# Two softmax attentions: attention values for two heads at once with V stationary, the result laid out by feature, and the divisors widened by GpSimd and turned by TensorE

## What is computed

```python
def _dsa_attention(...):            # layer 0, 8 heads; k_sel and v_sel are the 128 keys chosen for a query
    logits = jnp.einsum('bqhd,bqkhd->bhqk', qb, k_sel).astype(jnp.float32) * (dh ** -0.5)
    logits = jnp.where(valid[:, None], logits, -jnp.inf)
    p = jax.nn.softmax(logits, axis=-1).astype(v.dtype)
    return jnp.einsum('bhqk,bqkhd->bqhd', p, v_sel).reshape(bsz, Q_BLOCK, h * dh)
```

## Time and profile before

| | |
|---|---|
| three runs | 1926.04, 1927.58, 1929.67 us, median 1927.58 |
| profiled execution: own time | 1927.2 us |
| profiled execution: span | 1925.5 us |
| PE, PEld busy | 1843.1 and 1490.8 us |
| DVE, ACT, POOL busy | 892.6, 744.9 and 618.5 us |
| first attention | 839.8 to 887.6 us of the span |
| second attention | 1391.5 to 1510.2 us of the span, its eight turned tiles included |

### The profile page before, as it was taken

How to read it: one execution, slowest core, us unless ns; L and a number is a source line. 1 busy time by engine, 2 the same in 40 slices (tenths; PEclk the granted TensorE clock), 3 DMA queues, 4 the chain that set the end, 5 groups by cost and what they waited for, 6 DMA issues and landing times.

```text
span 1925.5 us, 22691 instructions
## 1 busy us (share of the span) xinstructions
PE 1843.1 (96%) x9025; PEld 1490.8 (77%) x9025; DVE 892.6 (46%) x1341; ACT 744.9 (39%) x1236; POOL 618.5 (32%) x203
## 2 busy tenths in 40 slices
PE   7999999998989999999999999998999999999998
PEld 4887777676777767878878888877778887888886
DVE  6411466555947258953442223345266253223334
ACT  3324655444334243344432222236544343232232
POOL 1433222222114323411434434334300243344332
PEclk8999999998999999999999999999999999999999
DMA  7533231211131312311222232322300122222321
GB/s 281 202 109 99 66 88 35 77 54 56 45 109 51 120 45 85 101 45 55 74 102 87 90 106 87 100 87 75 109 1 1 55 88 88 100 97 87 108 89 77
DMA packets 83379, 165.11 MB, mean 86 GB/s; under 512 B 5977, under 2 KB 8158, under 8 KB 83294
## 3 DMA queue, kind: packets, MB, share of 16 engines
q1 hardware_dynamic: 83294, 163.95, 25.9%
HBM read 157.64 MB, written 2.10 MB: 83 GB/s over the span
## 4 chain that ended last, share of the span: by engine, by line
PE 87%; DVE 7%; ACT 3%; issue 1%; POOL 1%; DMA 0%; SPq 0%; DVEq 0%; ACTq 0%
PE PDT L622 13%; PE PDT L624 12%; PE PDT L623 12%; PE PDT L633 9%; PE PDT L635 9%; PE PDT L634 9%; PE PM L1201 3%; PE PM L975 2%; PE PM L1171 1%; PE PDT L1171 1%; PE PM L942 1%; PE PM L1150 1%; PE PM L990 1%; PE PM L668 1%; PE PDT L760 1%
## 5 line engine op out<-in xcount | busy, mean ns | idle before, releaser
L1787 POOL TENSOR_TENSOR wlo<-wraw,whi 128x2048 fp32r<-128x2048 f32 (+4 forms) x154 | 606.6, 3945 | 1272.7 <-ACT whi L1304 1232.5
L1304 ACT ACTIVATE whi<-wraw 128x2048 fp32r<-128x2048 f32 (+2 forms) x133 | 247.8, 1863 | 554.1 <-PE PDT L624 320.4
L633 PE MATMUL PDT<-hhi,whi 128*128 128x512 f32 x800 | 316.2, 395 | 5.0 <-ACT mh_r L1423 5.0
L635 PE MATMUL PDT<-hhi,wlo 128*128 128x512 f32 x800 | 313.0, 391 | 0.0
L634 PE MATMUL PDT<-hlo,whi 128*128 128x512 f32 x800 | 313.0, 391 | 0.0
L622 PE MATMUL PDT<-whi,hhi 128*128 128x512 f32 (+1 forms) x612 | 242.9, 397 | 7.5 <-DVE hlo L1892 5.3
L623 PE MATMUL PDT<-wlo,hhi 128*128 128x512 f32 (+1 forms) x612 | 236.2, 386 | 0.0
L624 PE MATMUL PDT<-whi,hlo 128*128 128x512 f32 (+1 forms) x612 | 236.1, 386 | 0.0
L622 PE MATMUL PDT<-whi,mh_hi 128*128 128x512 f32 x512 | 202.5, 396 | 0.0
L624 PE MATMUL PDT<-whi,mh_lo 128*128 128x512 f32 x512 | 202.5, 396 | 0.0
L623 PE MATMUL PDT<-wlo,mh_hi 128*128 128x512 f32 x512 | 202.4, 395 | 0.0
(11 more groups left out here) (344 smaller groups left out, 2507.0 us busy)
## 6 DMA issues: line engine op xcount, KB each, us to landing
wraw<-in_mlp_w SPq DMA_DIRECT2D x64, 1024.0 KB, 5.2
wraw<-in_w_in SPq DMA_DIRECT2D x26, 1024.0 KB, 5.2
wraw<-in_even_w_in SPq DMA_DIRECT2D x16, 1024.0 KB, 5.3
w_ada<-in_w_ada SPq DMA_DIRECT2D x12, 1024.0 KB, 14.0
wraw<-in_w_out SPq DMA_DIRECT2D x8, 1024.0 KB, 5.1
swapped<-qk_sb SPq DMA_DIRECT2D x16, 256.0 KB, 6.6
wraw<-in_even_w_out SPq DMA_DIRECT2D x4, 1024.0 KB, 5.1
wraw<-in_odd_w_o SPq DMA_DIRECT2D x4, 1024.0 KB, 5.2
```

The costliest lines, as they stand in the source:

```text
L633: mm(bank, sth, hi[:, k0 + k, :], start=start and k == 0, stop=False)
L635: last = mm(bank, stl, hi[:, k0 + k, :], start=False, stop=stop and k == 3)
L1304: nc.scalar.activation(whi[base % 2][:, 0:n], wraw[base % 2][:, 0:n], ACT.Copy).then_inc(S("w_hi"), 1)
L1787: part = g.tensor_tensor(wlo[base % 2][:, cols], wraw[base % 2][:, cols], fl(whi[base % 2][:, cols]), ALU.subtract)
```

## The change

In both softmax attentions V is now the stationary operand, 64 columns of it, and the turned probabilities move. Two heads of a pair write partitions 0 to 63 and 64 to 127 of `PM` bank 3, so that a pair's result is already a feature tile of 512 tokens. A pair takes eight products: those of key tiles 1, 3 and 2 in an odd iteration h (`pair_values` with keys 1, 3, 2), that of key tile 0 (512 columns) in the next one. `turn_probs` puts the ten blocks in another order, four `prt` buffers take the place of two.

The divisors: DVE inverts `den` (`invert`), GpSimd spreads each over 64 columns (`widen`), four PE transposes turn a pair's (`turn_den`), ACT copies them to SBUF (`turned_den`), and DVE multiplies `PM` bank 3 by them (`over_den`), once a pair. `lat_high` (ACT) and `lat_low` (DVE) make `hhi` and `hlo` of the pair's tile. The turning of the result after each loop (`transposes`, `split_tiles`) goes. On ACT the copy of the turned probabilities comes after the first two of a head's four exponentials, not after all four. The load of `row_b` for layer 1 is moved behind the second attention, where one `prt` buffer now uses its place.

```diff
+    prt3 = [arena(f"prt3{s}", [P, 1280], kb) for s, kb in enumerate((21, 91, 96))]
+    prt3.append(at("prt33", [P, 1280], offset=place["row_a"]))
@@ -1181,29 +1196,39 @@
 
             X = PX[n % 2]
             pe.wait_ge(S("att_exps"), 4 * n + 4)
-            at_block = 0
             for t in (3, 2, 0, 1):
                 for j in range(t + 1):
-                    last = nc.tensor.transpose(X[:, at_block // 4, (at_block % 4) * P:(at_block % 4) * P + P],
-                                               p[n % 2][:, QB_FIRST[t] + j * P:QB_FIRST[t] + j * P + P], ident[:, :])
-                    at_block += 1
+                    at_column = KEY_FIRST[j] + (t - j) * P
+                    b, c0 = at_column // SEQ, at_column % SEQ
+                    a = QB_FIRST[t] + j * P
+                    last = nc.tensor.transpose(X[:, b, c0:c0 + P], p[n % 2][:, a:a + P], ident[:, :])
             last.then_inc(S("att_turned"), 1)
...
-        def values(n, pt, v):
-
-            c0 = 256 * (n % 2)
-            probs_taken(n + 1)
-            if n:
-                pe.wait_ge(S("att_out"), n)
+        def turn_den(pair, wide):
+
+            pe.wait_ge(S("den_wide"), 2 * pair + 2)
+            pe.wait_ge(S("tr_read"), den_group(pair))
             for t in range(TT):
-                for j in range(t + 1):
-                    a = QB_FIRST[t] + j * P
-                    last = mm(PM[:, 3, c0 + t * HD:c0 + t * HD + HD], pt[n % 2][:, a:a + P], v(j),
-                              start=j == 0, stop=j == t)
-            last.then_inc(S("att_pv"), 1)
+                last = nc.tensor.transpose(PDT[:, 3, t * P:t * P + P], wide[pair % 2][:, t, :], ident[:, :])
+            last.then_inc(S("tr_done"), 1)
+
+        def pair_values(pair, first, keys, pt, v):
+
+            if keys[0]:
+                probs_taken(2 * pair + 2)
+                if pair:
+                    pe.wait_ge(S("att_out"), pair)
+            for s in keys:
+                a, w = KEY_FIRST[s], SEQ - s * P
+                for half in range(2):
+                    c0 = (2 * (pair - first) + half) * HD
+                    last = mm(PM[HD * half:HD * half + HD, 3, s * P:SEQ], v[:, s, c0:c0 + HD],
+                              pt[(2 * pair + half) % 4][:, a:a + w], start=s == 1, stop=s == 0, skip_group_check=True)
+            if keys[0] == 0:
+                last.then_inc(S("att_pv"), 1)
 
...
+            if h >= 3 and h % 2:
+                pair_values((h - 3) // 2, 0, (1, 3, 2), prt, v2)
+                turn_den((h - 3) // 2, den_wide)
+            elif h >= 4:
+                pair_values((h - 4) // 2, 0, (0,), prt, v2)
...
         pe.wait_ge(S("conv2_done"), 4)
         wo2 = pieces("wo2", 1)
-        piece(*wo2[0])
-        pe.wait_ge(S("att_out"), A_H)
-        for n in range(3):
-            transposes("attn", n + 1 + n // 2, lambda t, k: v2[:, t, k * P:k * P + P], n)
-            piece(*wo2[n + 1])
-        transposed("attn", 4)
+        pe.wait_ge(S("tr_read"), TR["den2"][0] + A_H // 2)
+        for p in wo2[:4]:
+            piece(*p)
+        pe.wait_ge(S("attn_low"), KT + A_H // 2)
         for p in wo2[4:]:
             piece(*p)
...
             if n >= 4:
-                act.wait_ge(S("att_out"), n - 3)
-            for q, t in enumerate((3, 2, 0, 1)):
+                act.wait_ge(S("den_wide"), n - 3)
+            for q, t in order:
@@ -1689,19 +1717,36 @@
 
         def turned(n, pt):
             act.wait_ge(S("att_turned"), n + 1)
-            if n >= 2:
-                act.wait_ge(S("att_pv"), n - 1)
-            nc.scalar.activation(pt[n % 2][:, 0:SEQ], PX[n % 2][:, 0, :], ACT.Copy).then_inc(S("probs_s"), 1)
-
-        for h in range(A_H + 1):
+            if n >= 4:
+                act.wait_ge(S("att_pv"), n // 2 - 1)
+            nc.scalar.activation(pt[n % 4][:, 0:SEQ], PX[n % 2][:, 0, :], ACT.Copy).then_inc(S("probs_s"), 1)
+
+        def turned_den(pair):
+
+            act.wait_ge(S("tr_done"), den_group(pair) + 1)
+            if pair >= 2:
+                act.wait_ge(S("attn_low"), KT + pair - 1)
+            nc.scalar.activation(lat[pair % 2][:, :], PDT[:, 3, :], ACT.Copy).then_inc(S("tr_read"), 1)
+
+        def lat_high(pair, k):
+
+            act.wait_ge(S("att_out"), pair + 1)
+            nc.scalar.activation(hhi[:, k, :], lat[pair % 2][:, :], ACT.Copy).then_inc(S("attn_high"), 1)
...
-        for h in range(C_H + 1):
...
             if h < C_H:
-                exps(A_H + h, pr3, mx3, den3)
-            if h:
-                turned(A_H + h - 1, prt3)
+                exps(n, pr3, mx3, den3, ((0, 3), (1, 2)))
+            if 1 <= h <= C_H:
+                turned(n - 1, prt3)
+            if h < C_H:
+                exps(n, pr3, mx3, den3, ((2, 0), (3, 1)))
+            if h >= 5 and h % 2:
+                lat_high((n - 5) // 2, (h - 5) // 2)
+            if h >= 3 and h % 2 and h < C_H + 3:
+                turned_den((n - 3) // 2)
         hi(0, PH["wo3"][0] + 1, 0)
-        split_tiles("lat", 8, lambda k: 1.0, 0, "wo3")
...
+        def widen(n, d, wide):
+
+            pair, c0 = n // 2, HD * (n % 2)
+            pool.wait_ge(S("den_ready"), n + 1)
+            if pair >= 2:
+                pool.wait_ge(S("tr_done"), den_group(pair - 2) + 1)
+            g.tensor_copy(wide[pair % 2][:, :, c0:c0 + HD], d[:, n % 4, :].unsqueeze(2).to_broadcast([P, TT, HD]))\
+                .then_inc(S("den_wide"), 1)
+
+        for n in range(A_H):
+            widen(n, den, den_wide)
...
+        def invert(n, d):
+
             dve.wait_ge(S("att_exps"), 4 * n + 4)
-            link(v.reciprocal(d[:, n % 4, :], d[:, n % 4, :]))
-            dve.wait_ge(S("att_pv"), n + 1)
-            v.tensor_tensor(dst, PM[:, 3, 256 * s:256 * s + 256].rearrange("p (t d) -> p t d", t=TT),
-                            d[:, n % 4, :].unsqueeze(2).to_broadcast([P, TT, HD]), ALU.mult).then_inc(S("att_out"), 1)
-
-        dve.wait_ge(S("causal_made"), 2)
-        for h in range(A_H + 2):
+            v.reciprocal(d[:, n % 4, :], d[:, n % 4, :]).then_inc(S("den_ready"), 1)
+
+        def over_den(pair):
+
+            dve.wait_ge(S("att_pv"), pair + 1)
+            dve.wait_ge(S("tr_read"), den_group(pair) + 1)
+            o = lat[pair % 2][:, :]
+            v.tensor_tensor(o, PM[:, 3, :], o, ALU.mult).then_inc(S("att_out"), 1)
+
+        def lat_low(pair, k):
+
+            dve.wait_ge(S("attn_high"), KT + pair + 1)
+            v.tensor_tensor(hlo[:, k, :], lat[pair % 2][:, :], fl(hhi[:, k, :]), ALU.subtract).then_inc(S("attn_low"), 1)
...
-        for h in range(C_H + 2):
+        for h in range(C_H + 4):
+            n = A_H + h
+            pair = (n - 5) // 2 if h >= 5 and h % 2 else None
+            if pair is not None:
+                over_den(pair)
             if h < C_H:
-                row_least(A_H + h, mx3, lambda t: causal[:, (3 - t) * P:SEQ])
+                row_least(n, mx3, lambda t: causal[:, (3 - t) * P:SEQ])
             if 1 <= h <= C_H:
-                turned(A_H + h - 1, prt3)
+                turned(n - 1, prt3)
             if h + 2 < C_H:
                 turned_k(h + 2)
-            if h >= 2:
-                emit(A_H + h - 2, den3, v3[:, :, (h - 2) * HD:(h - 1) * HD])
-        split_tiles("lat", 8, lambda k: 1.0, 0)
+            if 1 <= h <= C_H:
+                invert(n - 1, den3)
+            if pair is not None:
+                lat_low(pair, pair - A_H // 2)
```

More of the change, by code:

```diff
@@ L242, in build_program @@
     pr = [arena("pr0", [P, 1280], 8), arena("pr1", [P, 1280], 13)]
-    prt = [arena("prt0", [P, 1280], 18), arena("prt1", [P, 1280], 23)]
+    prt = [arena(f"prt{s}", [P, 1280], kb) for s, kb in enumerate((18, 23, 60.5, 69.5))]
+    lat = [at(f"lat{s}", [P, SEQ], offset=place["junk"] + 2 * KB * s) for s in range(2)]
+    den_wide = [arena(f"den_wide{s}", [P, TT, 2 * HD], 28 + 2 * s) for s in range(2)]
     mx = arena("mx", [P, 4, TT], 77.625)
@@ L298, in build_program @@
     QB_FIRST = {3: 0, 2: 512, 0: 896, 1: 1024}
+    KEY_FIRST = {0: 0, 1: 512, 3: 896, 2: 1024}
     def kmajor(w):
@@ L389, in gate_at, with head_group, den_group @@
         return za[:, (k + 4) % KT, :]
+    def head_group(h, m):
+        return TR["heads"][0] + 2 * h + m + max(0, (h - 4) // 2)
+    def den_group(pair):
+        if pair < A_H // 2:
+            return TR["den2"][0] + pair
+        pair -= A_H // 2
+        return TR["heads"][0] + 2 * min(C_H, 2 * pair + 6) + pair
     def idx_pair(t, tile):
@@ L574, in _ @@
         mlp("mlp0", 0)
-        sp.wait_ge(S("post_mix0"), TT)
-        load(row_b[:, :], norm_mix_post_2[1].partition_broadcast(P), "row_b_loaded")
         sp.wait_ge(S("ffn0_made"), TT)
@@ L591, in _ @@
         columns("wo3", w_oo_v, 2, 0)
-        sp.wait_ge(S("tr_read"), TR["lat"][0])
+        sp.wait_ge(S("att_out"), (A_H + C_H) // 2)
+        load(row_b[:, :], norm_mix_post_2[1].partition_broadcast(P), "row_b_loaded")
         load(row_c[:, :], norm_ffn_pre_2[1].partition_broadcast(P), "row_pre")
@@ L1268, in _ @@
```

(39 more changed lines are left out.)

50 lines of the change are left out of this document (25 added, 25 removed).

## The result

The changed kernel takes 1909.28 us (median of four runs, 1907.02 to 1910.15) against 1926.82 for the kernel before on the same chip (1926.04 to 1929.67): a ratio of 0.9901 with a 95% interval of 0.9887 to 0.9914. Measured a second time beside the last experiments it took 1907.93 against 1930.48: 0.9887 (0.9871 to 0.9902). The two gains, 17.5 and 22.6 us, lie on either side of the 20.1 forecast.

A forecast was written before the change was run, and what follows sets the result against it. PE, working in 96% of the span, was taken to bound the kernel. Gains 16.2 (second attention) + 4.2 (first) - 0.3 (widen) = 20.1 from 1927.2 gave 1907.1, put at 1907.5 us for the median; range 1903 to 1914.

The forecast's parts named there:

- A: Whole kernel: the case as worked from PE's time in both attentions, 1907.5 us, own range 1903 to 1912; chance 0.70.
- Second attention, 16.2 forecast: Second attention: gain of 16.2 us, with head 15's logits 9.9 earlier and 6.3 at its end.
- the pair, 1.40 forecast: Second attention's loop: each pair of iterations gains 0.30 + 1.10 = 1.40 us, two heads taking 11.3 instead of 12.7.
- PE waits 0.16 for ACT's copy: Second attention, even iterations: ACT's copy ends at L+5.23, next logits at L+5.27; PE alone needs 5.11, so waits 0.16.
- what the forecast said of the reorder: Second attention: with ACT's copy still after four exponentials, L+6.02 would hold and even iterations gain 0.3 only.
- First attention, 4.2 less 0.3 forecast: First attention: gain 2.1 up to head 7 and 2.1 at the end, less 0.3 for widen slowing DVE.
- DVE's backlog: First attention: lat_low waits for lat_high in iteration 5, delaying head 6's minima and copy; head 7 comes 1.9 late.
- The collision: First attention: widen on GpSimd slows DVE's convolution step behind invert, costing 0.2 to 0.4 on DVE's late stretch.
- B: Both loops: softmax chain bounds them, pairs lose most of their 1.40; gain only 12, 1915.5 us; chance 0.13.
- C: Changing the array's form costs 0.6 a visit, 1919.5 us; if halves do not overlap, 1926; chance 0.10.
- D: Short PE waits keep a loop's clock at 1.2 GHz; slower by tens of us, 1935 for 33; chance 0.04.
- a sign of being wrong: Loops of both attentions: a granted clock below 1.00 within them was listed as showing the forecast wrong.

The follow-up runs named there:

- e9: The changed kernel, unchanged, measured and profiled a second time: 1907.93 us against 1930.48 for the kernel before, ratio 0.9887.
- e3: Kernel before with only ACT's copy of the turned probabilities moved behind two of the four exponentials: 0.998 of the kernel before.
- e4: Changed kernel with all eight products of a pair in the odd iteration and none in the even one: 0.9943 of the kernel before.
- e2: Changed kernel with ACT's copy of the turned probabilities behind all four exponentials again: 1919.75 us, 0.9951 of the kernel before.
- e6: Changed kernel with an odd iteration's six products ordered one head after the other, not in turn: 0.9951 of the kernel before.
- e7: Changed kernel with first attention's lat_low moved behind the next iteration's two convolution steps on DVE: 0.9898 of the kernel before.
- e12: Changed kernel with e10's order at the ends, wo3's first unit waiting only for tiles 0 to 3, and e7's edit: 1905.06 us, 0.9875 of before.
- e10: Changed kernel with products, over_den, last inversion and last turn_den reordered at the end of both attentions: 0.9877 of the kernel before.
- e8: Changed kernel with every widen made five times, one behind the other, on GpSimd: 0.9899 of the kernel before.
- e5: Changed kernel with divisors' transposes between the products of key tile 1 and tiles 3, 2, one more form visit per odd iteration: 0.9914 of before.
- e1: The kernel before, unchanged, profiled once more: 1930.81 us, where its median was 1929.74 on that chip.

## Why the forecast held, step by step

The forecast was 1907.5 by A, and 1909.28 was measured. Of its 20.1, the stages at full clock give 20.1 too, but from parts of other sizes: the second attention gave 0.9 less than forecast and the first 0.9 more. That the sum is met so closely is luck; each part is right to about 1 us.

- **Second attention, 16.2 forecast, 15.3 measured.** Head 1 to head 15 gave 9.15 for 9.9. The step that was mis-sized is the pair, 1.40 forecast and 1.23 measured: the entry into the 64-column form costs 0.2 before the first weights, where I had spread 0.07 a part (odd 6.16 for 6.07), and in the even iteration PE alone needs 5.34 (4.33 + 1.01) where I had 5.11. The end was 13.85 for 13.7. The start at full clock is 8.43 and 8.37 (e9, e3), no change: what it showed more in the first profile, 11.41 for 10.93, is clock.
- **"PE waits 0.16 for ACT's copy" in the even iterations did not come true.** The copy ended as forecast (L+5.21 for 5.23), but PE's own work was 0.23 longer than forecast and ends last, by 0.08 (e4: 5.26 without its products there). That 5.34 lies so near 5.27 is luck. The copy is the next bound right under it, and in its old place it is the bound: shown by e2 (L+6.00, 6.06). So what the forecast said of the reorder holds. That PE is the slower in the odd ones is borne out by e4 and e6, where more time on PE there lengthens them one for one.
- **First attention, 4.2 less 0.3 forecast, 4.8 measured** (47.88 to 44.89, and the 16 transposes between the pieces of wo2, 1.8: from weight load to weight load the four pieces took 12.65 and now 10.83; the forecast's 12.87 ran from a weight load to a product). DVE's backlog was mis-sized: 1.9 forecast, 0.7 measured. `lat_high` ended at L+6.42 and not at L+6.9, and minima and copy of head 6 took 2.7 and not 3.1. The odd iteration was mis-sized the other way, 5.62 for 5.37, by the two gaps of the form. Removing the backlog alone kept only 0.17 of it (e7), since the end of the stage took it back; with the end in another order it gives 0.67 (e12 against e10).
- **`widen`: 0.40** alone, by 0.5 assumed, and hidden (e8). The collision came as forecast on a convolution step behind `invert` (0.89 for 0.66 at 864.37 us), but not in the late stretch for which I had counted 0.3: there, in iteration 5, `widen` took its plain 0.40 while DVE waited for `lat_high`.
- **B** is refuted for ACT's and DVE's added work: the loop's pairs lose none of it. Its core, that ACT's queue decides half the iterations, was in A, and it missed by only 0.08.
- **C**: 0.15 a visit (e5) where it asked for 0.6, and the halves overlap (e6). The Trainium skill ("TensorEngine Tiling (Array Packing)", § Key Properties) lets different tiles work in parallel; the runs agree, and e6 shows that the order of the products decides how much of it comes about.
- **D**: no loop stayed at 1.2 GHz; in the first profile both loops had 1.00 throughout. But single spells did come inside loops, which I had called a sign of being wrong: in the first attention of e9 (0.50 and 0.65, 1.6 us) and of the kernel before (e1, 3.25), and at head 2 of the second attention in e10. At the start of the second attention they cost 3 us where they came.

The profiled executions differ by 17.4 only: 20.1, less 2.08 upstream, 0.5 at the second start and 0.35 behind wo3, and 0.2 gained between the attentions; of the upstream shift 1.56 is the spell shown under e1, and the start is clock too (e9); the rest was not looked into.

## What to carry to other kernels

When products are made cheaper in a software pipeline, ask at once which copy the next step waits for, and whether it can stand earlier in its engine's queue: here that reorder was worth 0.8 us alone and 5.6 with the change. Balance the two iterations of a pair before saving entries into a form: one group in place of two spares a visit and lost 0.78 a pair. At the seams between stages, check for each wait which tiles the first products really use (2.3 us), and before moving work into a gap of PE, see in the timeline that PE is idle there.

## What the hardware showed that I had not expected

- Two column halves of the array ran side by side, but how much depended on the order in the queue: the same six products took 1.44 us interleaved and 2.14 us one half after the other, where they overlapped only around the place at which the halves met.
- Around the 64-column form the weight loads stand still 0.17 to 0.18 on entering and 0.39 on leaving, but one more visit costs only 0.15 in all.
- GpSimd and DVE slowed each other where a `widen` met a DVE instruction with two SBUF inputs: `widen` took 0.78 for 0.40, and `lat_low` or a convolution step behind it 0.88 to 0.90 for 0.66 to 0.69; in the loop of the second attention, where most of DVE's inputs lie in PSUM, DVE's time stayed the same under five times the widening (e8).
- With PE busy 1.90 of the same 4 us ahead of it, one execution of the changed kernel granted 0.51 and 0.63 at the start of the second attention, and another 1.00.
